# Input products of a long convolution as split halves in a two-layer encoder kernel

## The reference

```python
xn = rmsnorm(x, norm_mix[l])
proj = xn @ w_in[l]
q, k, v, hy, g_a, g_h = jnp.split(proj, splits, axis=-1)
y_a = window_attention(rope(q), rope(k), v, sink) @ w_attn_branch[l]   # 8 heads of 64, window 128
x0, x1, vv = jnp.split(short_conv(hy), 3, axis=-1)    # hy: 3 x 512 channels
z = x1 * vv
y_h = (x0 * (irfft(rfft(z) * rfft(filter)) + z * skip)) @ w_hyena_branch[l]
merged = sigmoid(g_a) * y_a + sigmoid(g_h) * y_h
x = x + merged @ w_out[l]
x = x + peer_ffn(rmsnorm(x, norm_ffn[l]), ...)        # 16384 experts, the 16 best of 8 heads
```

## Time and profile before

| | us |
|---|---|
| median of 3 runs | 3435.19 |
| lowest, highest | 3433.8, 3437.17 |
| the profiled execution | 3436.2 |
| its span, first to last instruction | 3434.0 |
| TensorE busy | 3375.3 |
| stage of the change, layer 0 | about 114 to 250 |
| the same stage, layer 1 | about 1809 to 1944 |

### The profile page before, as it was taken

How to read it: one execution, slowest core, us unless ns; L and a number is a source line. 1 busy time by engine, 2 the same in 40 slices (tenths; PEclk the granted TensorE clock), 3 DMA queues, 4 the chain that set the end, 5 groups by cost and what they waited for, 6 DMA issues and landing times.

```text
span 3434.0 us, 47304 instructions
## 1 busy us (share of the span) xinstructions
PE 3375.3 (98%) x16086; PEld 2754.1 (80%) x16086; DVE 2636.8 (77%) x5503; ACT 1239.7 (36%) x1980; POOL 809.4 (24%) x661
## 2 busy tenths in 40 slices
PE   7999999999999999999999999999999999999998
PEld 4458855898888988888855688559988888998887
DVE  3574389997888888888736734999978888888888
ACT  2333223794223223333214322338833333223332
POOL 0000026002333333333300000440033333333332
PEclk9999999999999999999999999999999999999999
DMA  4313313468888888888741132144698888888885
GB/s 122 104 37 92 120 36 124 164 252 315 318 304 303 305 303 307 305 308 309 261 155 37 37 104 100 44 140 181 246 354 307 309 307 304 302 306 306 304 306 202
DMA packets 270646, 750.58 MB, mean 219 GB/s; under 512 B 19741, under 2 KB 139293, under 8 KB 243904
## 3 DMA queue, kind: packets, MB, share of 16 engines
q1 hardware_dynamic: 196768, 480.57, 39.6%
q0 software_dynamic: 73760, 268.47, 22.7%
HBM read 681.86 MB, written 67.11 MB: 218 GB/s over the span
## 4 chain that ended last, share of the span: by engine, by line
PE 81%; DVE 14%; DMA 2%; POOL 1%; ACT 1%; issue 1%; SPq 0%; DVEq 0%; POOLq 0%; ACTq 0%
PE ps L1239 29%; PE ps L1225 22%; PE ps L1029 7%; PE ps L898 4%; PE ps L1122 4%; DVE OHS L2143 3%; PE ps L1087 3%; PE ps L876 2%; DVE OHS L2139 2%; PE ps L1205 2%; PE ps L1176 2%; DVE URAWL L2109 1%; PE ps L1008 1%; PE ps L843 1%; DMA ROWS<-v_rows_dram,GIS 1%
## 5 line engine op out<-in xcount | busy, mean ns | idle before, releaser
L778 POOL DMA_INDIRECT ROWS<-v_rows_dram,GIS x256 | 331.4, 1294 | 576.2 <-DVE X L2213 483.7
L778 POOL DMA_INDIRECT ROWS<-u_rows_dram,GIS x256 | 300.8, 1175 | 609.6 <-DVE STG L2197 541.8
L1578 ACT ACTIVATE AC<-ps 128x384 f32<-128x384 f32 x192 | 94.4, 492 | 926.5 <-PE ps L1225 926.5
L1239 PE MATMUL ps<-VHI,WHI 128*128 128x512 f32 x1536 | 414.9, 392 | 6.6 <-DVE WLO L2178 3.7
L1239 PE MATMUL ps<-VLO,WHI 128*128 128x512 f32 x1536 | 415.3, 392 | 0.0
L1239 PE MATMUL ps<-VHI,WLO 128*128 128x512 f32 x1536 | 411.4, 390 | 0.0
L1571 ACT CAST VHI<-VRAW 128x512 fp32r<-128x512 f32 x512 | 285.8, 619 | 327.0 <-PE ps L1239 327.0
L2213 DVE SCALAR_TENSOR_TENSOR X<-ROWS,STG,X 128x1024 f32<-128x1024 f32 x256 | 328.2, 1282 | 22.8 <-DMA ROWS<-v_rows_dram,GIS 10.8
L1239 PEld LDWEIGHTS ps<-VLO,WHI 128*128 128x128 f32 x1536 | 288.8, 188 | 63.7
L1239 PEld LDWEIGHTS ps<-VHI,WLO 128*128 128x128 f32 x1536 | 288.6, 188 | 62.2
L1239 PEld LDWEIGHTS ps<-VHI,WHI 128*128 128x128 f32 x1536 | 285.6, 188 | 55.8 <-DVE WLO L2178 4.8
(11 more groups left out here) (281 smaller groups left out, 5351.1 us busy)
## 6 DMA issues: line engine op xcount, KB each, us to landing
VRAW<-v_dram SPq DMA_DIRECT2D x128, 1024.0 KB, 7.2
URAW<-ut_dram SPq DMA_DIRECT2D x128, 512.0 KB, 5.5
URAW<-ut_dram SPq DMA_DIRECT2D x64, 1024.0 KB, 5.8
g_table<-GST SPq DMA_DIRECT2D x12, 4096.0 KB, 12.9
GT<-g_table SPq DMA_DIRECT2D x62, 768.0 KB, 8.2
WR<-w_in_dram SPq DMA_DIRECT2D x8, 2048.0 KB, 12.0
WR<-w_in_dram SPq DMA_DIRECT2D x32, 512.0 KB, 4.7
WR<-w_q_dram SPq DMA_DIRECT2D x8, 2048.0 KB, 8.1
```

The lines of the kernel that those rows point to most:

```text
L778: pool.indirect_dma_start(out=ROWS[:, k % GR, :], out_offset=None, in_=table, in_offset=bass.IndirectOffsetOnAxis(ap=GIS[:, par, k:k + 1], ...
L1239: last = nc.tensor.matmul(ps[:, 2 + o, :], a[:, par, jj, b * P:(b + 1) * P], c[:, dh, jj, :], start=(first and n == 0), stop=(final and n ...
```

## The change

Products 3 to 11 of `hyena_in` are made of halves, 24 passes each. The high half of the activations goes to a new tensor `XHA` in slot 0 of the ring, copied by ScalarE once the filter's spectra are out; the low half `XL`, in the place of `XNT`, is subtracted by GpSimd after product 2. The weights of a product get their high half by ScalarE (into the place of the queries, or of `PT` and `FT`), their low half by VectorE in their place in the ring. Later in the layer `XH` is copied from `XHA`. The ring is reordered: tile 6 in slot 1, 7 in slot 2, 8 in slot 1. The mask and the maximum are one instruction per head.

```diff
...
+HY_SPLIT = 3
+HY_SPLITS = NHY - HY_SPLIT
+def slot_of(t):
+    return {T_HY + 2: 1, T_BR: 2, T_BR + 1: 1}.get(t, t % RING)
 def tile_uses():
...
             continue
-        got[t % RING] += 16 * parts[t]
-        out.append((t % RING, got[t % RING]))
+        got[slot_of(t)] += 16 * parts[t]
+        out.append((slot_of(t), got[slot_of(t)]))
     return out
...
     assert at[0] <= pt_at + 16 * HW and 4 * 4 * NB * (QH + KVH) * ROT <= 16 * HW
+    XHA, _ = sb("XHA", [P, KC, SEQ], F32R, offset=wr_at)
+    QKVL, _ = sb("QKVL", [P, NB, HY0], F32R, offset=qkv_at)
+    PTH, _ = sb("PTH", [P, KC, P], F32R, offset=pt_at + 16 * HW)
+    FTH, _ = sb("FTH", [P, KC, P], F32R, offset=ft_at)
...
     IN_ATT, IN_YH = (ATT[:], ATTH[:], ATTL[:]), (YH[:], YHH[:], YHL[:])
-    IN_X = [tuple(t[:, 4 * i:4 * i + 4] for t in (XNT, XH, XL)) for i in range(2)]
+    IN_X = [tuple(t[:, 4 * i:4 * i + 4] for t in (XNT, XHA, XL)) for i in range(2)]
+    def input_weights(n):
+        part = (slice(None), slot_of(T_HY + n // 4))
+        w, lo = (t[part].rearrange("p (b k n) -> p b k n", b=2, n=512)[:, :, :, (n % 4) * P:(n % 4 + 1) * P] for t in (WR, WRL))
+        if n < HY_A:
+            hi = QKVL[:, 2 * (n % 2):2 * (n % 2) + 2, 0:AW].rearrange("p b (k c) -> p b k c", c=P)
+        else:
+            hi = (PTH, FTH)[n - HY_A][:].rearrange("p (b k) c -> p b k c", b=2)
+        return w, hi, lo
...
-        part = (slice(None), (T_BR + n) % RING, slice((16, 0, 8)[i] * P, ((16, 0, 8)[i] + 8) * P))
+        part = (slice(None), slot_of(T_BR + n), slice((16, 0, 8)[i] * P, ((16, 0, 8)[i] + 8) * P))
         return WR[part], WCH[:, n % 2, i, :], WRL[part]
...
-        part = (slice(None), (T_OUT + half) % RING, slice(i * 1024, (i + 1) * 1024))
+        part = (slice(None), slot_of(T_OUT + half), slice(i * 1024, (i + 1) * 1024))
         return WR[part], WOH[half][:, i, :], WRL[part]
...
             def load_hyena(l, i):
-                part = at_cols(0, KC, 512)(WR[:, (T_HY + i) % RING, :])
-                sp.dma_start(part, cols_of(l, w_in, HY0 + 512 * HY_PARTS[i], 512)).then_inc(w_loaded[(T_HY + i) % RING], 16)
+                part = at_cols(0, KC, 512)(WR[:, slot_of(T_HY + i), :])
+                sp.dma_start(part, cols_of(l, w_in, HY0 + 512 * HY_PARTS[i], 512)).then_inc(w_loaded[slot_of(T_HY + i)], 16)
...
                     loaded[0] += 1
-                    sp.wait_ge(*tile_done[t - RING])
+                    if t == T_BR + 2:
+                        sp.wait_ge(in_hi, 5)
+                        sp.wait_ge(hy_out, NHY)
+                    else:
+                        sp.wait_ge(*tile_done[max(p for p in range(T_Q, t) if slot_of(p) == slot_of(t))])
                     for dst, src in parts:
-                        sp.dma_start(dst(WR[:, t % RING, :]), src).then_inc(w_loaded[t % RING], 16)
+                        sp.dma_start(dst(WR[:, slot_of(t), :]), src).then_inc(w_loaded[slot_of(t)], 16)
...
                 sp.wait_ge(kf_out, 2 * NF)
+                sp.wait_ge(*tile_done[T_HY])
                 load_hyena(l, 2)
...
                 pool.memset(HYT[:, :, SEQ + 1:SEQ + 2], 0.0).then_inc(pads_zero, 1)
+                pool.wait_ge(hy_out, HY_SPLIT)
+                for i, (x, hi, lo) in enumerate(IN_X):
+                    pool.wait_ge(in_hi, i + 1)
+                    nc.gpsimd.tensor_tensor(lo, x, hi.bitcast(F32), ALU.subtract).then_inc(in_split, 1)
                 tree = 0
...
                         pe.wait_ge(hy_copied, before[-1] + 1)
-                    w = WR[:, t % RING, :].rearrange("p (k n) -> p k n", n=512)
-                    for k in range(KC):
-                        last = nc.tensor.matmul(ps[:, bank, :], w[:, k, (n % 4) * P:(n % 4 + 1) * P], XNT[:, k, :],
-                                                start=(k == 0), stop=(k == KC - 1))
+                    if n < HY_SPLIT:
+                        w = WR[:, slot_of(t), :].rearrange("p (k n) -> p k n", n=512)
+                        for k in range(KC):
+                            last = nc.tensor.matmul(ps[:, bank, :], w[:, k, (n % 4) * P:(n % 4 + 1) * P], XNT[:, k, :],
+                                                    start=(k == 0), stop=(k == KC - 1))
+                    else:
+                        if n == HY_SPLIT:
+                            pe.wait_ge(in_split, 2)
+                        pe.wait_ge(wb_split, n - HY_SPLIT + 1)
+                        _, hi, lo = input_weights(n)
+                        for i, (w, xs) in enumerate(((hi, XHA), (lo, XHA), (hi, XL))):
+                            for k in range(KC):
+                                last = nc.tensor.matmul(ps[:, bank, :], w[:, k // 4, k % 4, :], xs[:, k, :],
+                                                        start=(i == 0 and k == 0), stop=(i == 2 and k == KC - 1))
                     last.then_inc(hy_out, 1)
...
                 HH, HL, LH = (0, 0), (0, 1), (1, 0)
-                pe.wait_ge(in_split, 1)
-                pe.wait_ge(wb_split, 1)
+                pe.wait_ge(in_split, 3)
+                pe.wait_ge(wb_split, HY_SPLITS + 1)
                 three(0, branch_pairs(0, 0, 0, 4, ATTH, ATTL))
-                pe.wait_ge(in_hi, 2)
-                pe.wait_ge(wb_split, 2)
+                pe.wait_ge(in_hi, 4)
+                pe.wait_ge(wb_split, HY_SPLITS + 2)
                 gate_part(1, 4, HH, True, False)
                 gate_part(1, 4, LH, False, False)
-                pe.wait_ge(wb_hi, 3)
+                pe.wait_ge(wb_hi, HY_SPLITS + 3)
                 gate_part(2, 4, HH, True, False)
-                pe.wait_ge(in_split, 2)
                 gate_part(1, 4, HL, False, False)
                 gate_part(2, 4, HL, False, False)
-                pe.wait_ge(wb_split, 3)
+                pe.wait_ge(wb_split, HY_SPLITS + 3)
                 gate_part(2, 4, LH, False, False)
-                pe.wait_ge(in_hi, 3)
+                pe.wait_ge(in_hi, 5)
                 for i in (1, 2):
...
                     gate_part(i, 0, LH, False, False)
-                pe.wait_ge(in_split, 3)
                 for i in (1, 2):
...
                         if k0 == 0:
-                            pe.wait_ge(wb_split, 3 * n + i + 1)
+                            pe.wait_ge(wb_split, HY_SPLITS + 3 * n + i + 1)
                         last = three(4 * (n % 2) + bank, branch_pairs(n, i, k0, nk, xh, xl))
...
+                def input_high(n):
+                    if n >= HY_SPLIT + 2 and n < HY_A:
+                        act.wait_ge(hy_out, n - 1)
+                    need_tile(act, T_HY + n // 4)
+                    high(*input_weights(n)).then_inc(wb_hi, 1)
+                act.wait_ge(kf_out, 2 * NF)
+                for i in range(2):
+                    high(*IN_X[i]).then_inc(in_hi, 1)
                 probs(0)
+                input_high(HY_SPLIT)
                 hyena_copy(HY_ROPE)
+                input_high(HY_SPLIT + 1)
                 act.wait_ge(hs_stored, 16)
...
                         hyena_copy(HY_ROPE + u + 1)
+                    if HY_SPLIT + u + 2 < HY_A:
+                        input_high(HY_SPLIT + u + 2)
                     attended(u)
...
                     nc.scalar.copy(ZTOK[:, g, :], ps[:, g, :]).then_inc(ztok_ready, 1)
+                input_high(HY_A)
                 for f in range(NF):
...
                     nc.scalar.copy(ZEV[:, f], ps[:, 4 - 4 * f:6 - 4 * f, :]).then_inc(zev_copied, 1)
+                act.wait_ge(zf_out, 2 * NF)
+                input_high(HY_A + 1)
                 for n in range(HY_A, NHY):
...
+                def keep_high(i):
+                    part = (slice(None), slice(4 * i, 4 * i + 4))
+                    nc.scalar.copy(XH[part], XHA[part].bitcast(F32)).then_inc(in_hi, 1)
                 act.wait_ge(yf_ready, 4)
...
                 branch_high(0)
-                high(*IN_X[1]).then_inc(in_hi, 1)
+                keep_high(1)
                 act.wait_ge(y_used, HC)
-                high(*IN_X[0]).then_inc(in_hi, 1)
+                keep_high(0)
                 high(*IN_YH).then_inc(in_hi, 1)
...
                         dve.wait_ge(probs_turned, kb_done[u - 2])
-                    mask = CST[:, C_MASK + m0:C_MASK + m0 + n].unsqueeze(1).to_broadcast([P, GROUP, n])
-                    nc.vector.scalar_tensor_tensor(SC[:, u % 2, :, 0:n], ps[:, 0:GROUP, 0:n], HD ** -0.5, mask,
-                                                   ALU.mult, ALU.add).then_inc(sc_copied, 1)
+                    mask = CST[:, C_MASK + m0:C_MASK + m0 + n]
+                    for h in range(GROUP):
+                        last = nc.vector.tensor_tensor_reduce(SC[:, u % 2, h, 0:n], ps[:, h, 0:n], mask, HD ** -0.5, NEG,
+                                                              ALU.add, ALU.max, accum_out=m[:, h:h + 1])
+                    last.then_inc(sc_copied, 1)
                     dve.wait_ge(sc_copied, u + 1)
-                    st.did(nc.vector.tensor_reduce(m, SC[:, u % 2, :, 0:n], axis=AX, op=ALU.max))
```

(24 more changed lines are left out.)

## The result

The changed kernel takes 3441.01 us (median of 16 runs, 3438.45 to 3445.03); the kernel before takes 3435.89 in as many (3433.56 to 3438.8). The ratio is 1.0014, with a 95% interval of 1.0007 to 1.002: no change by the bound of 0.2%, though the interval lies wholly on the slower side. 3437 was forecast.

What follows compares the result with a forecast made beforehand. TensorE, busy 98% of the span, was taken as the bound. Per layer -10.3 + 7.3 + 1.7 + 2.3 = +1.0 us, so +2.0 for both layers: 3437 us on the median, range 3427 to 3445.

Steps and rivals of the forecast that it cites:

- Products as split halves: Products 3 to 9 in the attention units: 24 passes replace 16, saving 1.47 us each, 10.3 us per layer.
- The wait for GpSimd: Ahead of product 3: TensorE waits for two GpSimd subtractions of 4.54 us, 7.3 us per layer, bounds 5.6 and 8.2.
- The clock: TensorE falls to half clock after the waits ahead of products 3 and 11, losing 1.7 us each per layer.
- Product 11: Its low half queues on VectorE: TensorE idles 3.4 us, product 11 ends 0.6 us later, losing products 10 and 11's savings.
- Fused form: Mask and running maximum on VectorE: 1.9 us for four heads instead of 3.5, keeping its loop hidden beside TensorE.
- The ring: Later loads of branch tiles and the third input tile still arrive before they are needed; cost nothing.
- (a): Waits cost less: GpSimd wait 5.6 us, no clock fall at product 11; -2.4 us per layer, 3430; chance 0.22.
- (b): GpSimd no bound: both subtractions some 4.6 us, clock stays up at products 3 and 11; 3421; chance 0.10.
- (d): GpSimd's output in the matmul's rounded format is slower, 7 us per subtraction; 3447; chance 0.08.
- (c): Fused maximum is dear, 3.8 us for four heads, so TensorE idles in the units; +6 per layer, 3447; chance 0.08.
- (e): The change doesn't do what it says: products in other passes than 24 of 0.227 us; chance 0.02.

Runs made afterwards that it cites:

- the run with busy waits: Changed kernel with unread matmuls filling TensorE's waits, 32 ahead of product 3 and 14 ahead of product 11; 3433.76 us.
- a_vector_low: Changed kernel with the activations' low half subtracted by VectorE in two instructions, none on GpSimd; 3431.72 us.
- d_wait_later: Changed kernel with product 3's wait for the activations' low half put ahead of its last eight passes only; 3433.1 us.
- e_unfused: Changed kernel with mask and maximum again as two instructions, the rest of the change kept; 3448.37 us.
- h_shared_low: Changed kernel with GpSimd subtracting the first half of the activations and VectorE the second, each right after product 2; 3436.57 us.
- c_low11_early: Changed kernel with product 11's low half moved on VectorE ahead of the second spectrum's sum and difference; 3435.05 us.
- the kernel with three cures: Changed kernel with VectorE subtracting, product 3's wait ahead of its last eight passes, and product 11's low half early; 3421.32 us, again 3422.82.

## Why the prediction was nearly right

The class (no change, towards slower) and the mechanism hold; the sizes of four terms add up to the difference. By the medians, which are 5.1 us apart, the forecast of +2 is 3 us short; the table is that of the profiled executions, where both layers make +7.1. Per layer, layer 0 / layer 1, in us:

| step | forecast | measured |
|---|---|---|
| products 3 to 9 | -10.3 | -9.7 / -9.5 |
| idle ahead of turned probabilities | 0 | -0.2 / +0.2 |
| wait for GpSimd | +7.3 | +7.6 / +7.8 |
| half clock behind it | +1.7 | +2.6 / +2.2 |
| product 10, product 11 and its wait | +0.6 | +0.9 / +0.9 |
| half clock behind that | +1.7 | +1.5 / +2.8 |
| sum | +1.0 | +2.7 / +4.4 |

Nearly all errors go the same way, so the sum did not come near by large errors that cancel. The clock terms come from the run with busy waits, the waits from the rows; the first line is what is left of the units (93.04 - 92.70 = 0.34 = 7.62 + 2.61 - 0.17 - 9.72), so it holds the error of the others.

- **Products as split halves.** I took the branches' pace, 1.81 us for eight passes. A product in a unit pays a start each time: 5.66 us for 5.44. From one product's start to the next the changed kernel takes 10.51 us (151.15 to 161.66), the kernel before 11.89, so a product saves 1.38 and not 1.47. The term is too large by 0.6 to 0.8.
- **The wait for GpSimd** was in its bounds. The sum has a slip of 0.1: 121.6 + 9.1 is 130.7, a wait of 7.2, and by the same steps the bounds are 5.4 and 8.1. Behind VectorE's low half, which ends at 120.32, both subtractions take 8.83 us (to 129.15), 4.42 each, a little under the 4.54 that I took. The rest is 0.5 us in which VectorE's own low half (119.10 to 120.32) held GpSimd up. That it did is read from the times: the first row of 4 elements ends at 124.71, 4.39 behind 120.32, the second with GpSimd. In layer 1 the row has 10.18 for the two, of which 8.82 lie behind the end of VectorE's low half at 1821.12, and 1.3 ahead of it. I had looked at GpSimd holding up VectorE, not at the reverse, and had read the earlier trace rows as a fourfold slowing, where in these runs VectorE waits for the end of GpSimd's instruction; nothing on the path hung on that.
- **The clock** is the step most off: 3.4 a layer forecast, 4.1 and 5.0 measured. The mechanism was right: the earlier trace rows gave its price from one fall, 1.7, and what followed such waits here cost from 0 to 2.9. It is in part luck that the two falls of a layer came out no further from 3.4: the same 3.4 us ahead of product 11 cost nothing in four of ten cases.
- **Product 11.** Wait 3.4 forecast, 3.38 found. Products 10 and 11 save 2.5 us together, for the 2.8 that were counted, which makes 0.9 of 0.6.
- **Fused form.** 1.9 us forecast, 2.04 found; it is a condition of the gain. My figure that a unit would be late by 0.8 without it fits the 0.6 to 0.7 of the unfused run.
- **The ring** cost nothing: nothing waits for a weight load in the branches, as argued. (the earlier trace rows has 1.33 us as the longest issue; the 1.1 that I used is the median, and it changes nothing.)
- **Rivals.** (a) and (b) fell with the 4.42 us per subtraction, (d) as well; (c) fell with the 2.04; (e) with 24 passes seen. The other half of (a), no fall of the clock ahead of product 11, did come in both layers of the unfused kernel and in one layer of two others.

What stays open: why a given idle spell of 3.4 us costs nothing in one layer and 2.9 us in another. Filling the waits shows what the falls cost, not what picks their length.

## What to carry to other kernels

A saving spread over many products can be eaten whole by one wait at their head: ask which pass is the first to need the late operand, and put the wait there. Move the subtraction to the engine that does it in half the time, in pieces between that engine's urgent work. Where TensorE must idle for some us, put a price range on its clock and not one price: here 3.4 us cost 0 to 2.9, 2.3 us cost 0 or 1.6, and 1.1 us cost nothing.

## What the runs showed of the hardware

**VectorE and GpSimd exclude each other in these rows, even for tiny instructions.** An instruction of 4 elements with two SBUF inputs took 1.54 and 4.42 us beside GpSimd's subtraction, and 0.16 alone; the latter ended with GpSimd's. The fused form, with one input in PSUM, took 0.42 per head beside GpSimd as without it. In the run with shared work GpSimd's subtraction took 7.11 us: it got through only after VectorE's 2.29 us instruction, and needed its 4.4 from there. The Trainium skill, page SBUF — State Buffer, section Who interferes with whom, says that a VectorE instruction with two SBUF inputs contends with a GpSimd instruction that reads SBUF, that the shared ports are an exclusive lock, and that the order of issue decides who is blocked. The trace agrees on the lock, with these numbers. On the order it does not show the same: GpSimd's recorded start is the earlier one at 1819.76 (VectorE 1819.90) and at 119.88 (VectorE 120.34), and VectorE went first both times. Whether the recorded start is the moment at which GpSimd asks for its inputs is open. By the lock a delay of GpSimd by up to VectorE's 1.22 us instruction could have been forecast.

**GpSimd's price.** The Trainium skill, page GPSIMD Engine Reference, section Performance versus the Vector engine, has 4497 ns against 2293 for VectorE, for a two-input instruction of 2048 float32 elements. The trace agrees within 2%: 4.42 and 2.29 us, with an output of type `fp32r`.

**The clock after an idle spell.** Of ten waits of 3.38 to 3.40 us ahead of product 11 (the changed kernel, a_vector_low, d_wait_later, e_unfused and h_shared_low, two layers each), four were followed by full clock (tail 42.7 us, as with busy waits, 42.6), five by a loss of 1.5 (tail 44.1 to 44.2), one by 2.9 (45.51). Ahead of product 3, by its time against the 5.7 us of the run with busy waits, six waits of 7.6 to 7.9 us (the changed kernel, c_low11_early, e_unfused) cost 2.0 to 2.7, those of 3.20 and 3.43 us (a_vector_low) 1.5 and 2.6, those of 5.37 and 5.58 us (h_shared_low) 2.5 and 1.6: the loss does not grow with the wait. In the kernel with three cures 2.11 us idle cost nothing, 2.33 and 2.34 us cost 1.6 in its two profiles, while 2.34 cost nothing in the earlier trace rows. Waits of 1.1 us ahead of product 11 cost nothing in any of eight cases.
